# Attention intermediates of VectorE kept in PSUM, a normalisation spread between reductions, and a narrower weight split, in a two-block transformer kernel on Trainium2

## What is computed

```python
u = h @ w_in
c_q, c_kv, k_rope, z = jnp.split(u, [384, 640, 672], axis=-1)
q  = (rmsnorm_2(c_q, q_norm) @ w_q_b).reshape(B, S, 16, 64 + 32)
q_rope = apply_rope(q[..., 64:], cos[:, :, None], sin[:, :, None])
kv = (rmsnorm_2(c_kv, kv_norm) @ w_kv_b).reshape(B, S, 16, 64 + 64)
for blk in range(S // 128):
    s = (q_nope . k_nope + q_rope . k_rope) * scale      # keys up to the block's end
    prob = softmax(where(k_chunk <= q_chunk, s, -inf))
    outs.append(prob @ v)
return (o * silu(z)) @ w_out
```

## Time and profile before

| | us |
|---|---|
| median of 3 runs | 2222.67 (2220.42 to 2224.28) |
| profiled execution, its own time | 2225.34 |
| profiled execution, span | 2223.5 |
| PE busy | 2064.3 (93%) |
| PEld busy | 1657.0 (75%) |
| DVE busy | 1109.1 (50%) |
| POOL busy | 1095.0 (49%) |
| ACT busy | 673.4 (30%) |

### The profile page before, as it was taken

The page is one execution under the profiler, slowest core; times in us unless marked ns, Lnnn a source line. Parts: engine busy times, 40 slices in busy tenths (PEclk is TensorE's granted clock), DMA queues, the critical chain, the costliest instruction groups (busy, mean ns, idle before and its releaser), DMA issues.

```text
span 2223.5 us, 26435 instructions
## 1 busy us (share of the span) xinstructions
PE 2064.3 (93%) x9488; PEld 1657.0 (75%) x9488; DVE 1109.1 (50%) x1189; ACT 673.4 (30%) x1085; POOL 1095.0 (49%) x651
## 2 busy tenths in 40 slices
PE   5999999989999999999999998997999999989996
PEld 3777767877788788788878876886777777768774
DVE  6545556465631212112111278314888888863576
ACT  3345564222221000000000032112666666650312
POOL 1545555414734633633443373334666666654373
PEclk9999999989999999999999998997999999989997
DMA  3100001103211211211111121111000000001122
GB/s 136 49 20 20 19 10 38 38 29 117 83 47 47 76 47 47 77 46 50 63 53 51 48 95 47 48 49 38 19 21 19 19 19 19 19 29 47 48 76 95
DMA packets 31641, 106.64 MB, mean 48 GB/s; under 512 B 3449, under 2 KB 3641, under 8 KB 31577
## 3 DMA queue, kind: packets, MB, share of 16 engines
q1 hardware_dynamic: 27520, 96.14, 13.1%
q10 hardware_dynamic: 4066, 9.74, 1.2%
HBM read 101.51 MB, written 4.26 MB: 48 GB/s over the span
## 4 chain that ended last, share of the span: by engine, by line
PE 66%; POOL 10%; DVE 10%; issue 10%; ACT 3%; ACTq 0%; DMA 0%; POOLq 0%; DVEq 0%
PE ps L225 49%; POOL probs_lo L684 7%; PE ps L390 4%; PE ps L242 3%; PE ps L254 2%; POOL w_lo L1938 2%; POOL w_hi L1936 1%; DVE h_lo L371 1%; PE ps L628 1%; DVE tmp L1764 1%; DVE x L1766 1%; PE ps L635 1%; DVE S_all L1296 1%; PE ps L629 1%; PE ps L616 1%
## 5 line engine op out<-in xcount | busy, mean ns | idle before, releaser
L1936 POOL TENSOR_TENSOR w_hi<-w_raw,zero 128x1024 fp32r<-128x1024 f32 (+1 forms) x173 | 333.9, 1930 | 820.6 <-PE ps L225 579.5
L1938 POOL TENSOR_TENSOR w_lo<-w_raw,w_hi 128x1024 fp32r<-128x1024 f32 (+1 forms) x173 | 432.9, 2502 | 13.6
L225 PE MATMUL ps<-h_hi,w_lo 128*128 128x512 f32 x1328 | 334.8, 394 | 5.3 <-DVE x L517 5.1
L225 PE MATMUL ps<-h_hi,w_hi 128*128 128x512 f32 x1328 | 328.0, 389 | 0.0
L225 PE MATMUL ps<-h_lo,w_hi 128*128 128x512 f32 x1216 | 300.4, 389 | 0.0
L225 PEld LDWEIGHTS ps<-h_hi,w_lo 128*128 128x128 f32 x1328 | 249.4, 189 | 60.3 <-issue 9.3
L684 POOL TENSOR_TENSOR probs_lo<-probs,mla_p_hi 128x512 fp32r<-128x512 f32 x192 | 218.2, 1158 | 150.2 <-ACT probs L677 150.2
L225 PEld LDWEIGHTS ps<-h_hi,w_hi 128*128 128x128 f32 x1328 | 249.2, 188 | 51.8
L225 PEld LDWEIGHTS ps<-h_lo,w_hi 128*128 128x128 f32 x1216 | 228.4, 188 | 47.7
L1378 DVE TENSOR_TENSOR tmp<-ps,tmp 128x1024 f32<-128x1024 f32 x22 | 26.9, 1224 | 370.3 <-PE ps L225 363.6
L719 DVE TENSOR_REDUCE mx<-ps 128x1 f32<-128x128 f32 (+1 forms) x192 | 137.4, 751 | 79.8 <-PE ps L660 48.9
(11 more groups left out here) (341 smaller groups left out, 3738.4 us busy)
## 6 DMA issues: line engine op xcount, KB each, us to landing
w_raw<-in_wpack SPq DMA_DIRECT2D x173, 512.0 KB, 3.2
x<-in_xT ACTq DMA_DIRECT2D x16, 512.0 KB, 7.9
out<-result SPq DMA_DIRECT2D x8, 512.0 KB, 2.9
p_raw<-in_pT ACTq DMA_DIRECT2D x1, 1024.0 KB, 6.8
pos_i<-in_pos SPq DMA_DIRECT2D x1, 512.0 KB, 6.4
const_stage<-in_consts SPq DMA_DIRECT2D x1, 404.0 KB, 3.5
vec<-in_vecs SPq DMA_DIRECT2D x1, 284.0 KB, 4.4
mla_q_hi<-c_neg ACTq DMA_DIRECT2D x16, 4.0 KB
```

Of the source, the lines that this page charges most:

```text
L225: last = nc.tensor.matmul(dst[:, half, :], w[slot][:, kt, :], a[:, i, t], start=(n == 0), stop=(n == total - 1))
L1936: nc.gpsimd.tensor_tensor(w_hi[s][:, kts, :], raw[s][:, kts, :], no_change[:, kts, :], ALU.add).then_inc(w_hi_done, 1)
L1938: nc.gpsimd.tensor_tensor(w_lo[s][:, kts, :], raw[s][:, kts, :], w_hi[s][:, kts, :].bitcast(F32), ALU.subtract)\
```

## The change

It has four parts.

1. The normalisation writes `newton` back into PSUM (rows 64 to 127 of `O_BANK[half]`), and in MLA also the refined reciprocal; only the last factor before the final product is in SBUF (`rec`). The tile `newton` is gone. None of the four operations has two inputs in SBUF any more.
2. The rope of MLA's queries is made in place in PSUM (`q[CR]`), and `rope_x` is gone; L1687 and L1695 had both inputs in SBUF, and have one in PSUM now.
3. The first half's normalisation is cut into its four parts (`part` 0 to 3), put behind mx 3, mx 4, mx 5 and mx 6 (`NORM_BEHIND`), in FOX and MLA alike (FOX has no part 2). The second half's stays in one piece (`norm_whole_dve`).
4. POOL splits 5 of 8 tiles of an MLA head's weights. Its loop over heads ends one turn earlier, with the last two steps written out, since the last one splits a whole unit of the output projection.

```diff
+        NORM_BEHIND = {3: (0,), 4: (1,), 5: (2,), 6: (3,)}
...
-        newton = at("newton", R_W + 4096, [P, HALF])
...
+        def norm_half_dve(dve, A, n, b, half, tile, gate, part):
+            count = 3 if gate else 2
+            seq = n * (2 * count) + half * count
             rows = slice(HD * b, HD * b + HD)
+            sums, out = PS[HD:P, O_BANK[half], :], PS[0:HD, O_BANK[half], :]
             dst = flat(mix[rows, bass.ds(tile, 1), half * HALF:(half + 1) * HALF])
+            factor = rec[rows, :] if gate else rec[0:HD, :]
+            again = half == 1 or not (isinstance(n, int) and n == 0)
+            if part == 0:
+                dve.wait_ge(A.r0_done, n * 2 + (half + 1))
+                nc.vector.tensor_tensor(sums, sums, r0[0:HD, :], ALU.mult).then_inc(A.newton, 1)
+            elif part == 1:
+                dve.wait_ge(A.newton, seq + 1)
+                if again and not gate:
+                    dve.wait_ge(A.norm_done, n * 2 + half)
+                nc.vector.scalar_tensor_tensor(sums if gate else factor, sums, -2.0, r0[0:HD, :], ALU.add, ALU.mult).then_inc(A.newton, 1)
+            elif part == 2 and gate:
+                dve.wait_ge(A.newton, seq + 2)
+                if again:
+                    dve.wait_ge(A.norm_done, n * 2 + half)
+                nc.vector.tensor_tensor(factor, sums, dst, ALU.mult).then_inc(A.newton, 1)
+            elif part == 3:
+                dve.wait_ge(A.newton, seq + count)
+                nc.vector.scalar_tensor_tensor(dst, out, -1.0, factor, ALU.mult, ALU.mult).then_inc(A.norm_done, 1)
...
             for i in range(N_MAX):
                 max_dve(dve, A, n, i)
-                if i == 3 and prev is not None:
-                    norm_half_dve(dve, A, prev, 1 - b, 0, tile, gate)
+                if prev is not None:
+                    for part in NORM_BEHIND.get(i, ()):
+                        norm_half_dve(dve, A, prev, 1 - b, 0, tile, gate, part)
...
-                nc.scalar.activation(q_hi[b][CR, :], rope_x[CR, :], ACT.Copy).then_inc(mla.hi_done, 1)
+                nc.scalar.activation(q_hi[b][CR, :], q[CR, :], ACT.Copy).then_inc(mla.hi_done, 1)
...
-            nc.vector.tensor_tensor(rope_x[CR, :], q[CR, :], cos_sin[CR, :], ALU.mult).then_inc(mla.rope_done, 1)
+            nc.vector.tensor_tensor(q[CR, :], q[CR, :], cos_sin[CR, :], ALU.mult).then_inc(mla.rope_done, 1)
             nc.vector.tensor_tensor(rope_y[CR, :], q[SR, :], cos_sin[SR, :], ALU.mult).then_inc(mla.rope_done, 1)
             dve.wait_ge(mla.rope_done, n * 3 + 2)
-            nc.vector.tensor_tensor(rope_x[CR, :], rope_x[CR, :], rope_y[CR, :], ALU.add).then_inc(mla.rope_done, 1)
+            nc.vector.tensor_tensor(q[CR, :], q[CR, :], rope_y[CR, :], ALU.add).then_inc(mla.rope_done, 1)
...
-            nc.vector.tensor_tensor(q_lo[b][CR, :], rope_x[CR, :], q_hi[b][CR, :].bitcast(F32), ALU.subtract).then_inc(mla.lo_done, 1)
+            nc.vector.tensor_tensor(q_lo[b][CR, :], q[CR, :], q_hi[b][CR, :].bitcast(F32), ALU.subtract).then_inc(mla.lo_done, 1)
...
-                steps(pool, A, step)
+                last = A.heads // 2 - 1
+                for b in range(2):
+                    step(b, b, 0)
+                with pool.Fori(1, last) as turn:
+                    for b in range(2):
+                        step(turn * 2 + b, b, turn)
+                step(2 * last, 0, last)
+                step(2 * last + 1, 1, last, slice(0, DT))
...
-            heads(mla, U_HEAD)
+            heads(mla, U_HEAD, MLA_KTS)
```

More of the change, by code:

```diff
@@ L694, in rough_act @@
             nc.scalar.activation(r0[0:HD, :], ln_sum[0:HD, :], ACT.Exp, scale=-1.0).then_inc(A.r0_done, 1)
[L696 to L700, removed]
+        def norm_half_dve(dve, A, n, b, half, tile, gate, part):
+            count = 3 if gate else 2
+            seq = n * (2 * count) + half * count
             rows = slice(HD * b, HD * b + HD)
[L702 to L709, removed]
-            dst = flat(mix[rows, bass.ds(tile, 1), half * HALF:(half + 1) * HALF])
[L711 to L714, removed]
@@ L716, in max_dve, with norm_whole_dve @@
+        def norm_whole_dve(dve, *which):
+            for part in range(4):
+                norm_half_dve(dve, *which, part)
         def max_dve(dve, A, n, i):
@@ L839, in step_dve @@
             if prev is not None:
-                norm_half_dve(dve, A, prev, 1 - b, 1, tile, gate)
+                norm_whole_dve(dve, A, prev, 1 - b, 1, tile, gate)
         def steps(eng, A, step):
@@ L1595, in build @@
         mla.n_lo = 3
-        rope_x = at("rope_x", R_W + 16384, [P, T])
+        MLA_KTS = (QL + KVL) // P
         rope_y = at("rope_y", R_W, [P, T])
@@ L1948, in units, with heads, step @@
                     split(end - 1, (end - 1) % 2, (end - 1) // 2 * 16 + 16, k)
-            def heads(A, first):
-                def step(n, b, turn):
+            def heads(A, first, kts):
+                def step(n, b, turn, k=slice(0, kts)):
                     u = first + b + 1
-                    split(turn * 2 + u, u % 2, turn * 16 + (u // 2 * 16 + 16))
+                    split(turn * 2 + u, u % 2, turn * 16 + (u // 2 * 16 + 16), k)
                     if not (isinstance(n, int) and n == 0):
@@ L1962, in _ @@
             fox_constants_pool(pool)
-            heads(fox, U_FQK)
+            heads(fox, U_FQK, DT)
             units(U_FQK + FOX_H + 1, U_DN[-1])
@@ L2022, in _ @@
             for half in range(2):
-                norm_half_dve(dve, fox, FOX_H - 1, 1, half, 4 + FOX_H // 2 - 1, False)
+                norm_whole_dve(dve, fox, FOX_H - 1, 1, half, 4 + FOX_H // 2 - 1, False)
             gla_dve(dve)
@@ L2030, in _ @@
             steps(dve, mla, lambda n, b, turn: step_dve(dve, mla, n, b, turn, mla_prepare_dve, 0, True))
-            norm_half_dve(dve, mla, MLA_H - 1, 1, 0, MLA_H // 2 - 1, True)
+            norm_whole_dve(dve, mla, MLA_H - 1, 1, 0, MLA_H // 2 - 1, True)
             for k in range(2):
                 mix_lo_dve(dve, k, k, m2_hi, m2_lo)
-            norm_half_dve(dve, mla, MLA_H - 1, 1, 1, MLA_H // 2 - 1, True)
+            norm_whole_dve(dve, mla, MLA_H - 1, 1, 1, MLA_H // 2 - 1, True)
             for k in range(2, DT - 1):
```

## The result

| | before | changed |
|---|---|---|
| median, us | 2223.48 (2220.42 to 2226.17) | 2191.16 (2189.24 to 2192.06) |
| profiled execution, its own time, us | 2225.34 | 2191.03 |
| profiled execution, span, us | 2223.5 | 2189.2 |

Four runs of each on one chip give a ratio of 0.9854, interval [0.9837, 0.9871]: 32.3 us in the medians, 34.3 between the two profiled spans, since the profiled execution of before was itself some 2 us over its median.

The account below looks back on a forecast made before the run. PE was taken as the bound, with time to win at its waits in MLA heads. Heads 30.5 us, plus 2.3 and 0.5, less 1.0, gave 32.3 gained: 2191 us; 8 in 10 within 2182 to 2207.

Parts of the forecast that it names:

- What bounds the kernel now: MLA heads: PE waits at four places, for POOL, ACT twice and DVE, losing 0.75 at piece 1 and 1.30 at mx 6.
- Rope in PSUM: MLA heads: POOL's piece 1 ends 0.98 earlier, PE's first wait goes, everything from piece 5 on is 0.95 us earlier.
- Rival B: MLA heads: ACT's chain doesn't move, PE meets the first wait again at pieces 4 and 5; 1.15 a head, 2204; 11%.
- rival C: MLA heads: ACT's head start also removes the waits at pieces 4 and 5; 3.1 us a head, 2176; 6%.
- Normalisation cut up: MLA heads at mx 6: mx 4 waits for one part instead of four; 1.41 us gained, 0.25 given back.
- Rival D: MLA heads: the waits aren't from two SBUF inputs and stay, only the order helps; 0.6 a head, 2214; 4%.
- Given back: MLA heads at L667, the row of maxima: part 3 stands before mx 7, so PE loses 0.25 us.
- Cost of writing to PSUM: DVE's operations: bounded between no more than now and a second column pass (1.22 for 512 instead of 0.69); lower end taken.
- A: DVE's writes to PSUM cost a second pass; 1.05 a head instead of 2.1, 2207; 8%.
- E: Slower: PSUM writes make DVE the bound; at two extra passes 1.45 a head, 21 us slower, 2244; 2%.
- Second half's normalisation: MLA heads, before the next rope: L708 and L712 no longer meet POOL, but there is slack towards ACT; nothing gained.
- Five tiles: MLA heads: POOL's split falls from 2.40 to about 1.5, but POOL then idles until ACT's first exponential; nothing gained.

Follow-up runs that it names:

- e1: The kernel before with only the MLA rope in PSUM; normalisation in SBUF and in one piece, eight tiles split: 2207.0 us, ratio 0.9927.
- e2: The kernel before with only the normalisation in PSUM, in one piece; rope in SBUF, eight tiles split: 2206.83 us, ratio 0.9926.
- e5: The changed kernel with the first half's normalisation in one piece behind mx 3: 2196.98 us, ratio 0.9875 to the kernel before.
- e4: The kernel before with only POOL's split cut to five tiles of an MLA head: 2219.3 us, ratio 0.9981.
- e3: The kernel before with the first half's normalisation cut up but in SBUF; rope in SBUF, eight tiles split: 2213.92 us, ratio 0.9958.
- e6: The changed kernel with part 3 behind mx 7 instead of mx 6, in MLA and FOX: 2186.08 us, ratio 0.9823 to the kernel before.
- e9: The changed kernel with eight tiles of an MLA head split again: 2191.51 us, ratio 0.9856 to the kernel before.

## Why the prediction was right, and where its steps were not

2191 was predicted, 2191.16 measured, with a head of 24.7 predicted and 24.79 measured. The forecast's mechanism holds. Its steps in turn:

- *What bounds the kernel now* (four places where PE waits, DVE and POOL taking turns): right. e1, e2 and e5 each move the place that they should, and the held operations fall to the time of the unheld ones. The Trainium skill, "SBUF — State Buffer", section "Who interferes with whom", has the rule: a VectorE instruction with two SBUF inputs and a GpSimd instruction that reads SBUF exclude each other for whole instructions, one with a single SBUF input (outside VectorE's 2-port modes) doesn't take part, and the order of issue decides who blocks. The traces agree on all three: 2.21 and 1.24 for the rope's sum with two and with one, 1.49 and 1.01 for POOL's piece, and 1.22 for the sum in e4, which has two but came first.
- *Rope in PSUM*, 0.95: right to the hundredth in e1. Rival B falls, since the waits for ACT moved along and did not grow (0.32 at piece 5 in e1), and rival C, since they did not go either.
- *Normalisation cut up*, 1.41 less 0.25: nearly right as a sum for this place, with the wrong name. By e2 and e5 more than half is PSUM's: part 2 at 0.69 instead of 1.55 takes 0.70 of the 1.30, and the cutting up only the remaining 0.6, of which 0.3 comes back at L669. That share depends on which is taken first, since e3, with the order alone, takes the whole wait at mx 6 and 0.85 a head: both remove the same stall. The prediction saw that L712 was held (1.55) but put the whole place under the order of the list. Rival D said that only the order helps; e2, with the old order, disproves it.
- *Given back* at the row of maxima, 0.25: the term was too small. The column of waits shows 0.32, but e6 gets 0.43 a head back, and from the transposes to the next projection PE takes 1.01 and 1.13 in two heads in a row, against 0.56 and 0.70 in e6: some 0.44.
- *Cost of writing to PSUM*: the lower end was right, 14 ns an operation and none for a second pass. Rivals A and E fall. The errata table of "VectorE: DVE Perf Modes" in the Trainium skill would have made it an estimated 65 ns for an operation with a PSUM source. By L705 (693 ns in the mean over these heads before) and L708's shortest, 682, the source costs 11 ns; the target costs 14.
- *Second half's normalisation*, nothing, and *Five tiles*, nothing: the steps that failed. Both were costed by who waits for the end of that work. Their effect goes by another way: they set when DVE and POOL begin their next operations, so which of the two comes first at the rope. In the kernel before, that is 0.37 a head for either (e2's second wait, e4). In the whole change it is hidden, since the rope in PSUM takes the collision away in any case, so the two zeros, wrong as they were reasoned, left the sum right. For the five tiles e9 shows it; for the second half's normalisation inside the change no run does.
- The same overlap shows in the four parts taken alone: 17, 17, 10 and 5 us, some 50 in all, where together they bring 32. They remove the same stalls more than once.
- *FOX*, 1 us lost: right, 0.14 a head where 0.15 was said. The first split came 0.20 earlier in the changed kernel (145.00 against 145.20), and PE's return from its wait for `c_neg` in the last step 0.69 later (323.40 against 322.71): 0.9 for FOX. The other 0.8 of the 1.49 follows behind that wait and is the clock's (below). With part 3 behind mx 7 (e6) both are gone.
- *The end*, 2.3: L709 to L722 run without being held, 0.71, 0.71, 0.69, 0.69, which is the 2.3. But only 1.77 arrives, and the same in e2 (6.47 us for the stretch, against 8.24 to 8.25 in e1, e3 and e4). `mix_lo`, two SBUF inputs, is what comes next, and it now starts while POOL still splits: 1.73 for the first of five, against 1.21. 0.52 goes back there. The prediction should have asked here, as it did in the heads, what is late next.

```profile
L1037 DVE TENSOR_TENSOR mix_lo<-mix,h_hi x5: 1212/1212/1732, 1952.2 to 1957.2; 128x1024 fp32r<-128x1024 f32 x5
```

- *The last head's attention*, 0.5: 51.46 - 48.91 = 2.55, with 2.07 for the step 0.48 is left. This settles nothing: e9, with the same instructions there, needs 48.28, so two single executions differ by more. *The first step*, 1.05: 1.92. It gains nearly as much as the others; the half was a guess.
- Not in the sum at all: the clock's part (below), 1.5 us gained between FOX and MLA and 1.2 behind the end, and 0.8 lost at the end of FOX.

The misses are small and of both signs (+0.9 in the first step, -0.5 at the end, -0.4 in the 13 heads, +0.3 up to the end of FOX, +1.9 by the clock; in all +2, by which the two profiled spans differ more than the medians, 34.3 against 32.3), so that the closeness of 2191 is partly luck; the head's 2.07 against 2.1, which is nine tenths of it, is not.

## What to carry to other kernels

Where two engines exclude each other, an operation's price is also in when the next collision happens: before an edit is costed at nothing, ask whether it changes which of the two arrives first, and how small the present distance is (here 0.21 us). Giving one operand of DVE a home in PSUM removed the exclusion for 14 ns an operation, and after that the length of POOL's split no longer mattered (e9). When parts of a change are tried alone, their gains don't add up where they remove the same stall, so the whole and its leave-one-out versions (e5, e9) say more of what each is worth in place.
